# Mixture-of-experts output: rows added in place in DRAM by accumulating scatters, instead of a combine stage

## The reference

```python
def expert_block(args):                      # xblk: rows of one expert
    xblk, e = args
    return (jax.nn.silu(xblk @ w1[e]) * (xblk @ w3[e])) @ w2[e]
yb = lax.map(expert_block, (xb, block_e)).reshape(R, D)
out = jnp.zeros((T + 1, D), h.dtype).at[row_tok].add((yb * row_w[:, None]).astype(h.dtype))
```

## Time and profile before

| | us |
|---|---|
| median of 3 runs (lowest, highest) | 2693.58 (2692.51, 2702.32) |
| profiled execution, its own time | 2693.79 |
| its span, first to last instruction | 2692.0 |
| mean granted TensorE clock, of full | 0.948 |
| PE busy | 2370.7 (88%) |
| DVE, ACT, POOL busy | 1099.4, 751.0, 389.3 |

### The profile page before, as it was taken

How to read it: one execution, slowest core, us unless ns; L and a number is a source line. 1 busy time by engine, 2 the same in 40 slices (tenths; PEclk the granted TensorE clock), 3 DMA queues, 4 the chain that set the end, 5 groups by cost and what they waited for, 6 DMA issues and landing times. The chain is left out here.

```text
span 2692.0 us, 67585 instructions
## 1 busy us (share of the span) xinstructions
PE 2370.7 (88%) x27838; PEld 1461.3 (54%) x27839; DVE 1099.4 (41%) x2596; ACT 751.0 (28%) x1847; POOL 389.3 (14%) x480
## 2 busy tenths in 40 slices
PE   3999999999996899999999995589999999998960
PEld 1878777787875667777776773323232333232320
DVE  0355556565554355565655554311111111111118
ACT  0254454545443113222231321012121222211212
POOL 0112111111211112121222210000011111001000
PEclk8999999999997899999999997699999999999985
DMA  8011121211108432213222211845535496999959
GB/s 335 9 73 71 48 95 48 95 48 73 71 40 330 159 120 88 104 73 108 76 92 101 89 65 39 344 186 233 227 140 234 144 386 233 399 372 385 389 223 367
DMA packets 54676, 451.80 MB, mean 168 GB/s; under 512 B 7932, under 2 KB 8992, under 8 KB 32576
## 3 DMA queue, kind: packets, MB, share of 16 engines
q1 hardware_dynamic: 36504, 390.71, 36.9%
q0 software_dynamic: 10656, 38.80, 3.7%
q10 hardware_dynamic: 7304, 19.19, 1.9%
HBM read 367.41 MB, written 87.56 MB: 169 GB/s over the span
## 5 line engine op out<-in xcount | busy, mean ns | idle before, releaser
L1759 PE MATMUL ps<-arena 128*32 128x512 f32 x4608 | 507.4, 597 | 24.8 <-DMA arena<-wex 24.8
L453 PE MATMUL ps<-arena 128*128 128x128 f32 x3072 | 353.9, 275 | 13.5 <-ACT arena L593 13.5
L453 PEld LDWEIGHTS ps<-arena 128*128 128x128 f32 x3072 | 348.4, 192 | 26.3 <-ACT arena L593 26.3
L1759 PEld LDWEIGHTS ps<-arena 128*32 128x32 f32 x4608 | 149.6, 110 | 375.8 <-issue 361.3
L1099 PE MATMUL ps<-arena 64*64 64x64 f32 x8704 | 299.3, 222 | 30.0 <-issue 8.5
L1099 PEld LDWEIGHTS ps<-arena 64*64 64x64 f32 x8704 | 279.5, 137 | 59.0 <-issue 57.8
L1773 PE MATMUL ps<-arena 128*32 128x512 f32 x2304 | 265.6, 602 | 10.6 <-DMA arena<-wex 10.1
L1258 PE MATMUL ps<-arena 128*128 128x512 f32 x496 | 229.2, 605 | 0.7 <-ACT arena L1336 0.7
L1979 DVE TENSOR_TENSOR arena<-arena,ps 128x256 f32<-128x256 f32 x72 | 29.9, 415 | 458.3 <-ACT arena L1817 458.3
L464 PE MATMUL ps<-arena 128*128 128x512 f32 (+1 forms) x512 | 215.2, 559 | 0.0
L1817 ACT ACT_TABLE_LOAD x36 | 46.2, 1283 | 579.2 <-PE ps L1759 579.2
(11 more groups left out here) (331 smaller groups left out, 2841.8 us busy)
## 6 DMA issues: line engine op xcount, KB each, us to landing
arena<-wex SPq DMA_DIRECT2D x105, 2048.0 KB
mid<-arena SPq DMA_DIRECT2D x16, 2568.0 KB, 8.5
arena<-mid SPq DMA_DIRECT2D x16, 2568.0 KB, 9.7
arena<-ada SPq DMA_DIRECT2D x12, 2048.0 KB, 9.5
arena<-y SPq DMA_DIRECT2D x16, 1024.0 KB, 7.9
arena<-x SPq DMA_DIRECT2D x31, 512.0 KB, 5.5
arena<-w_in SPq DMA_DIRECT2D x8, 1232.0 KB, 24.9
arena<-x ACTq DMA_DIRECT2D x17, 512.0 KB, 10.5
```

The costliest lines, as they stand in the source:

```text
L453: mm = pe.matmul(bank[name][0:m, at:at + P], V["w_in"][:, kk, w0:w0 + m], V["hT"][:, kk, :], start=(kk == 0), stop=(kk == KD - 1))
L1759: mm = pe.matmul(bank[("HA", "HB")[g]][rows[j], :], xT[:, kk, rows[j]], slot[j][:, at:at + 2 * FH], start=(kk == 0), stop=(kk == KD - 1))
```

## The change

The output is summed where it lies. `x1` is stored straight into the output tensor, which gets 128 spare rows at its end. The weights of the rows travel through the same one-hot matmul as the tokens (`row_w`: the right-hand side is 82 instead of 41 columns wide). The eviction multiplies by the row's weight and the gate. Then POOL issues two indirect transfers a block that add in DRAM, one after the other: the first for rows that are a token's first choice (all others go to the spare rows), the second for the second choice. Behind `row_tok`, 18 more small DVE operations on 41 columns or fewer make `row_w`, `row0` and `row1` (all but the last left out below). `ysb` and the gate get places of their own in SBUF, for which the descriptor area shrinks to 8192 bytes a partition; ACT's wait for the scatter goes; scatter 0 goes; the combine stage goes.

```diff
@@ pass1, SP, ahead of the loop
+            sp.dma_start(dram["out"][T:T + P, :].rearrange("p (a n) -> p a n", a=4),
+                         V["S"].unsqueeze(1).to_broadcast([P, 4, CC * HD])).then_inc(S["spare_rows"], 16)
@@ pass2, SP
-                if i == MODS:
-                    sp.wait_ge(S["mod_added"], MOD1 + MODS)
-                    sp.dma_start(dram["gates"], W["gt2"]).then_inc(S["gates_out"], 16)
@@ experts, POOL
-            def scatter(b):
+            def add_rows(b):
                 pool.wait_ge(S["y_read"], b + 1)
-                pool.tensor_copy(W["idx_y"].bitcast(I32), W["row_y"][:, bass.ds(b, 1)])
+                pool.tensor_copy(W["idx0"].bitcast(I32), W["row0"][:, bass.ds(b - 1, 1)])
+                pool.tensor_copy(W["idx1"].bitcast(I32), W["row1"][:, bass.ds(b - 1, 1)])
                 pool.drain()
-                pool.indirect_dma_start(dram["y"], bass.IndirectOffsetOnAxis(ap=W["idx_y"], axis=0), W["ysb"],
-                                        None).then_inc(S["y_out"], 16)
+                pool.indirect_dma_start(dram["out"], bass.IndirectOffsetOnAxis(ap=W["idx0"], axis=0), W["ysb"], None,
+                                        compute_op=ALU.add).then_inc(S["added0"], 16)
+                pool.wait_ge(S["added0"], b * 16)
+                pool.sem_inc(S["pool_passed"], 1)
+                pool.indirect_dma_start(dram["out"], bass.IndirectOffsetOnAxis(ap=W["idx1"], axis=0), W["ysb"], None,
+                                        compute_op=ALU.add).then_inc(S["added1"], 16)
+                pool.wait_ge(S["added1"], b * 16)
+                pool.sem_inc(S["ysb_free"], 1)
             gather(0)
-            with pool.Fori(0, NB) as b:
+            pool.sem_inc(S["ysb_free"], 1)
+            pool.wait_ge(S["x_turned"], 1)
+            gather(1)
+            pool.wait_ge(S["row_out"], 1)
+            with pool.Fori(1, NB) as b:
                 with pool.If(b < nblk):
                     pool.wait_ge(S["x_turned"], b + 1)
                     gather(b + 1)
-                    scatter(b)
-            scatter(nblk)
+                    add_rows(b)
+            add_rows(nblk)
@@ experts, ACT
-                            act.wait_ge(S["y_out"], b * 16 + 16)
...
-            for t in range(NT):
-                act.dma_start(W["x1"][t], dram["x1"][P * t:P * t + P, :]).then_inc(S[f"x1_in{t // FLIGHT}"], 16)
@@ experts, DVE, the tables (4 turns)
-                dve.tensor_tensor(hi, hi, per_channel(W["tok_t"][:, cols], NB + 1), ALU.mult).then_inc(S["entries"], 1)
+                dve.tensor_tensor(hi[:, 1], hi[:, 0], per_channel(V["top_w"][:, cols], NB + 1), ALU.mult)
+                dve.tensor_tensor(hi[:, 0], hi[:, 0], per_channel(W["tok_t"][:, cols], NB + 1), ALU.mult).then_inc(S["entries"], 1)
...
             dve.tensor_scalar(W["row_tok"], W["row_tok"], 1, None, ALU.arith_shift_right).then_inc(S["row_tok"], 1)
...
+            dve.tensor_copy(W["row1"], W["vf"]).then_inc(S["row_out"], 1)
@@ experts, DVE, the eviction
+                    dve.tensor_copy(W["w_now"], W["row_w"][:, bass.ds(b, 1)])
+                    dve.drain()
+                    dve.wait_ge(S["ysb_free"], b + 1)
                     dve.wait_ge(S["phases"], b * PIECES + PIECES + 1)
                     for n0 in range(2):
-                        i = dve.tensor_copy(W["ysb"][:, 512 * n0:512 * n0 + 512], bank[f"Y{n0}"][:, :])
+                        i = dve.scalar_tensor_tensor(W["ysb"][:, cols], bank[f"Y{n0}"][:, :], W["w_now"][:, 0:1],
+                                                     W["gt2"][:, cols], ALU.mult, ALU.mult)
                     i.then_inc(S["y_read"], 1)
@@ program
-        combine(nc, S, V, W, dram)
```

More of the change, by code:

```diff
@@ L870, in views @@
     total = 53200
-    arena = ctx.enter_context(nc.sbuf_tensor("arena", [P, total], F32))
-    V = {}
+    arena = ctx.enter_context(nc.sbuf_tensor("arena", [P, total + 2 * D], F32))
+    V = {"gt2": arena[:, total:total + D], "ysb": arena[:, total + D:]}
     a = Arena(arena)
@@ L959, in views2 @@
     W = {n[1:]: v for n, v in V.items() if n[0] == "2"}
+    W["gt2"] = V["gt2"]
     for n in ("w_out", "w_router", "yT", "h2T"):
@@ L1583 @@
 SLOT = PIECES * PIECE
-FLIGHT = 4
 DUMP = LANES * SLOT - 2 * PIECE
@@ L1592, in views3 @@
     for name, w in (("xT", D), ("h", FE), ("hT", FE), ("xg", D), ("tok_t", 2 * NT), ("lof", 2 * NT), ("hif", 2 * NT),
-                    ("row_tok", NB + 1), ("row_y", NB + 1), ("idx_now", 1), ("idx_y", 1), ("need", 2 * PIECES * NB), ("load", 3 * NLOAD), ("nblk", 1)):
+                    ("row_tok", NB + 1), ("row1", NB + 1), ("idx_now", 1), ("idx0", 1), ("idx1", 1), ("w_now", 1), ("need", 2 * PIECES * NB), ("load", 3 * NLOAD), ("nblk", 1)):
         W[name] = a.take(w)
     h_at = V["keep_end"] + LANES * SLOT + D
[L1596 to L1603, removed]
+    tables_at = h_at + 2 * FE + D
+    W["row_w"] = arena[:, tables_at:tables_at + NB + 1]
+    W["row0"] = arena[:, tables_at + NB + 1:tables_at + 2 * (NB + 1)]
+    assert 2 * (NB + 1) <= 6 * NT
+    W["gt2"], W["ysb"] = V["gt2"], V["ysb"]
+    HOTS = 2 * COLS_PER_TURN * (NB + 1)
+    W["lo_hot"] = [split(w, COLS_PER_TURN) for w in (W["xT"], arena[:, h_at:h_at + 2 * FE])]
+    W["hi_hot"] = [w[:, 0:HOTS].rearrange("p (f c n) -> p f c n", f=2, c=COLS_PER_TURN) for w in (W["ysb"], W["xg"])]
+    W["tokf"], W["iota"] = W["xg"][:, HOTS:HOTS + NB + 1], W["xg"][:, D - P:]
+    assert COLS_PER_TURN * P <= D and HOTS + NB + 1 + P <= D and HOTS + 5 * (NB + 1) + 1 <= D
+    W["part"] = W["ysb"][:, D - 1:]
+    for i, name in enumerate(("vf", "codd", "tf", "dump", "unused")):
+        W[name] = W["ysb"][:, HOTS + (NB + 1) * i:HOTS + (NB + 1) * i + NB + 1]
     assert a.at <= total, a.at
-    for name in ("idx_now", "idx_y"):
+    for name in ("idx_now", "idx0", "idx1"):
         W[name] = W[name].bitcast(U32)
-    for name in ("row_tok", "row_y", "need", "load", "nblk"):
+    for name in ("row_tok", "row0", "row1", "need", "load", "nblk"):
         W[name] = W[name].bitcast(I32)
@@ L1633, in views3 @@
     assert a.at <= total, a.at
[L1636 to L1642, removed]
     return W
@@ L1683, in _ @@
             load(NLOAD // 2, 0)
+            for r in range(2):
+                sp.wait_ge(S[f"piece{r}"], 16 * PIECE_LOADS[r] + 16)
         @block.gpsimd
@@ L2051, in program @@
         scratch = lambda n, shape, dt=F32: nc.dram_tensor(n, shape, dt, kind="Internal").ap()
-        dram = {"x": ins["x"], "gates": scratch("gates", [P, D]), "bias": scratch("bias", [QH, CHUNK * (REL_PITCH + 1)]), "mid": scratch("mid", [NT, P, NPK]),
-                "x1": scratch("x1", [T, D]), "xn2": scratch("xn2", [T + 1, D]),
-                "y": scratch("y", [2 * T + P, D]), "out": out}
+        dram = {"x": ins["x"], "bias": scratch("bias", [QH, CHUNK * (REL_PITCH + 1)]), "mid": scratch("mid", [NT, P, NPK]),
+                "x1": out[0:T, :], "xn2": scratch("xn2", [T + 1, D]),
+                "out": out}
         setup(nc, S, ps, V, ins, dram)
@@ L2111 @@
     from concourse.bass_utils import run_bass_kernel_spmd
-    nc = bacc.Bacc("TRN2", target_bir_lowering=False, num_devices=1)
+    nc = bacc.Bacc("TRN2", target_bir_lowering=False, num_devices=1, dynamic_dma_scratch_size=8192)
     arrays = {n: np.ascontiguousarray(v) for n, v in host_arrays(inputs).items()}
     ins = {n: nc.dram_tensor(n, v.shape, mybir.dt.from_np(v.dtype), kind="ExternalInput").ap() for n, v in arrays.items()}
-    out = nc.dram_tensor("out", (T, D), F32, kind="ExternalOutput").ap()
+    out = nc.dram_tensor("out", (T + P, D), F32, kind="ExternalOutput").ap()
     program(nc, ins, out)
     result = run_bass_kernel_spmd(nc, [arrays], core_ids=[0])
-    return result.results[0]["out"].reshape(1, T, D)
+    return result.results[0]["out"][:T].reshape(1, T, D)
```

79 lines of the change are left out of this document (24 added, 55 removed).

## The result

| | us |
|---|---|
| predicted, with its range | 2648 (2610 to 2760) |
| measured, median of 4 runs (lowest, highest) | 2736.63 (2729.19, 2746.61) |
| before, beside it, median of 4 runs | 2693.27 |
| ratio, 95% interval | 1.0156 [1.0117, 1.0195] |
| span of the profiled execution, before and after | 2692.0, 2734.8 |

The change made the kernel slower, by 43 us or 1.6%. The forecast was faster. The direction was wrong.

What follows compares the result with a forecast made beforehand. The loop was taken as bound by PE, and by DMA where weights change, with the combine stage wholly on the path. 2692.0 - 74.3 + 24 + 8 - 5 + 1, plus 1.8 outside the span, gave 2647.5 us; range 2610 to 2760.

Steps and rivals of the forecast that it cites:

- The tail: After the last eviction: issue, two adds in series and program end take 12.1 us against 86.4, so -74.3 us.
- An ordinary block: Block loop without weight changes: POOL's new chain of 10.9 us from L1696 hides behind PE, cost 0.
- signs of being wrong: Add landing after 16 us (B) or 9 (C), DVE's eviction waiting over 10, PE's `wex` waits growing from 35 to over 60.
- A block that changes weights: Eight blocks with late scatters: the longer POOL chain makes the next gather 3 us late in each, +24 us.
- the adding: Each add: a scatter plus one read, 4.65 us to land; by the skill it would hold each engine 2.7 us.
- The added traffic delays weights: Blocks that change weights: the adds' extra DMA time lengthens PE's waits for weights, +8 us (0 to +32).
- ACT's wait: Block loop: removing ACT's wait for the scatter gives back at most 17.4 us; taken as -5 (0 to -17).
- The tables: Before the block loop: an extra DVE product per turn and wider matmuls, +1 us (-1 to +14).
- B: Where weights load, an add's second read queues like its own transfer, landing after 19.9 us; 2760 us, chance 0.17.
- C: In any block, a row's read and write don't overlap between rows, so POOL's chain bounds blocks; 2971 us, chance 0.07.

## Why the prediction was wrong

**The tail: right in kind, 3.4 us off in size.** It said 12.1 us behind the last eviction; it took 15.5. The term off is the add's landing, 4.65 us in the prediction, 6.0 at the least in the run; twice that difference is 2.7 of the 3.4.

**"An ordinary block": right that it costs nothing by itself, wrong in the margin.** The chain was to take 10.9 us from L1696, with the gather in flight beside it. When POOL is late, gather, drain and adds follow each other, and the chain takes 20.5 of 22.5 us from gather to gather. So a block that falls behind is hardly caught up in the next. One of the prediction's signs of being wrong came true here: DVE's eviction was to wait for POOL by no more than 10 us, and DVE stood idle up to 24.0 before one until POOL freed `ysb`.

**"A block that changes weights": this step failed.** The issue of the first add "4.5 us after L1696" was taken over from the kernel before as a fixed cost of such a block. It was a wait for the gather to land, at the drain. The gather of that block, on POOL's timeline of the kernel before:

```profile
2301.13 0.98 POOL L1691 DMA_INDIRECT arena<-xn,arena  x1 [0.86 <-issue]
```

It was issued 7.8 us ahead of the copy, so only some 4 us of its landing were left at the drain; the scatter's issue at 2313.31 is 12.2 us behind it, and a gather takes up to 12.0 to land. Once POOL is late, gather and copies follow each other at once, and the same drain costs the whole landing, 10.2 us. Three landings in series, not two, stand in a loaded block: 39.8 us where the prediction had 30.7 and the gather's issue. The landing of an add there was nearly right, 12.95 against a longest of 14.1. In place of 8 x 3 us the gather held PE for 70 us in 12 blocks. The run without that drain shows this cause, worth 44 us, the whole loss against the kernel before. It doesn't bring the forecast gain of 46 us; the runs with plain writes come near it or below it, so what stands in its way is the adding.

**The second part of that step, the adding.** The landing in a quiet block was put at a scatter plus one read, 4.65 us; it is 6.0 and more. An add holds each engine 3.24 us where 2.7 were assumed. By the Trainium skill (Collectives: The Full Stack, "The bandwidth ceiling: the fold count and why AG ≠ RS ≠ AR") two source reads halve the rate; on the prediction's 1.35 us that is an estimate of 2.7. The measurement decides: 2.3 times a plain write's 1.38. Plain writes in the same places give 71 to 79 us back.

**"The added traffic delays weights", +8: of the right size.** The sums hide it, 33.7 us against 34.9, because the first wait of the loop, 4.5 us for the first weights, stands under "wex" in the kernel before and under "issue" in the changed one. Behind it, PE waited for weights 30.4, 24.5 and 25.6 us in three traces of the kernel before (two of them with the small descriptor area or the 4 KB pattern, which changed nothing) and 33.7, 40.0 and 32.5 in three of the changed kernel: 8.6 us more in the mean. Whatever shortened the chain left longer waits for weights, 45.0 us without the drain and 57.0 with one add. That is a reason why 44 us from one edit and 79 from another need not add up; that the chain and the weights share one budget is argued, not shown.

**ACT's wait, -5:** removing a like wait in the kernel before gave nothing measurable. It should have been 0, as the block cited for it said.

**The tables, +1:** the loop starts 3.3 us later in this pair. In three traces each it starts between 1726.2 and 1735.8 us in the kernel before and between 1733.0 and 1736.4 in the changed one, so the term can't be told from nothing.

**The rivals.** B came nearest in direction, by the wrong path: it wanted landings of 16 us and more. In the changed kernel none took over 14.1 (15.0 in its repeat); the third landing in series did what B ascribed to a longer one. Nor does an add take two packets a row, which B had left open: the packets are as many as without the adding. The rule that it named (the Trainium skill, DMA: Bandwidth & Descriptors, "Queues, rings and completion order"), turns by packet, agrees with what the 4 KB packets did to the longest landing, 14.1 to 10.7 us. C did not happen: the median landing is 6.6 us, and C needed 9.4.

**Open:** why an add takes 2.3 times a plain write's engine time rather than 2. Three things were not tried: a second `ysb`, to free DVE, for which this kernel's layout leaves no room; the order in which no drain stands between any two transfers; and fewer rows per add. Each add moves all 128 rows of a block, 36 x 2 x 128 = 9216 in all, of which 2048 x 2 = 4096 are a token's; the rest go to the spare rows.

## What to carry to other kernels

Before moving work onto a queue, write its whole cycle down, every instruction in it, as gather, drain, add, wait, add, and give it the landing times of a loaded stretch; a queue that was half idle can still become the longest loop. A wait that looks like a constant in the kernel before may be the rest of a longer one that ran beside something else: ask what it waits for and when that was started. And where a chain is shortened in front of a full DMA system, look at the next wait before counting the gain.

## What the runs showed of the hardware that was not expected

- A drain on POOL behind an indirect transfer held the next indirect transfer until the first had landed: the add stood 212.3 us on issue with the drain between, 5.8 without; the scatter 70.0 and 0.3 in the kernel before. A drain between an add and a gather did the same, 149.8 us.
- An indirect add of 128 rows of 4 KB landed 6.0 us after issue at the least (5.8 in the run without the drain), a plain scatter 3.3; it held each DMA engine 3.24 us against 1.38, and POOL itself 1.59 us against 0.99. Both take 144 packets.
- Beside weights in 16 KB packets the first add's longest landing was 14.1 us, beside 4 KB ones 10.7, while its median rose from 6.6 to 8.6; the 4 KB packets cost the kernel before 0.5%.
- A pattern of 4 runs of 4 KB that lie side by side gave the packets of one run of 16 KB, 34440 in both.
